# Latent attention: keys of two heads in one product, query weights laid out anew, and the rotary swap in four 32-row corners

## What is computed

```python
MLA_HEADS, MLA_NOPE, MLA_ROPE = 8, 64, 32          # 96 query columns per head
Q_LORA, KV_LORA = 384, 256

def apply_rope(t, cos, sin):
    t1, t2 = jnp.split(t, 2, axis=-1)
    return jnp.concatenate([t1 * cos - t2 * sin, t2 * cos + t1 * sin], axis=-1)

def mla_branch(c_q, c_kv, k_r, cos, sin, q_norm_g, kv_norm_g, w_uq, w_uk, w_uv):
    q = (rmsnorm(c_q, q_norm_g) @ w_uq).reshape(B, S, 8, 96)
    q_nope, q_rope = q[..., :64], apply_rope(q[..., 64:], cos, sin)
    k_rope = apply_rope(k_r, cos, sin)              # one for all heads
    ckv = rmsnorm(c_kv, kv_norm_g)
    k_nope = (ckv @ w_uk).reshape(B, S, 8, 64)
    v = (ckv @ w_uv).reshape(B, S, 8, 64)
    return causal_mla_attention(q_nope, q_rope, k_nope, k_rope, v)
```

## Time and profile before

| | |
|---|---|
| median of 3 runs | 2799.29 us (2795.35 to 2803.37) |
| profiled execution | 2800.07 us, its span 2798.3 us |
| TensorE (PE) | 2739.1 us busy, 21992 matmuls |
| VectorE (DVE) | 1840.9 us busy, 66% |
| ScalarE (ACT) | 1301.3 us busy, 47% |
| GpSimd (POOL) | 70.8 us busy, 3% |
| DMA | 474.50 MB, mean 170 GB/s |

### The profile page before, as it was taken

How to read it: one execution, slowest core, us unless ns; L and a number is a source line. 1 busy time by engine, 2 the same in 40 slices (tenths; PEclk the granted TensorE clock), 3 DMA queues, 4 the chain that set the end, 5 groups by cost and what they waited for, 6 DMA issues and landing times.

```text
span 2798.3 us, 51128 instructions
## 1 busy us (share of the span) xinstructions
PE 2739.1 (98%) x21992; PEld 2601.1 (93%) x21992; DVE 1840.9 (66%) x3008; ACT 1301.3 (47%) x1860; POOL 70.8 (3%) x66
## 2 busy tenths in 40 slices
PE   8999999999999999999999999999999999999998
PEld 8999799999999989999999888899999998878997
DVE  5678676666676666766666557666666654766675
ACT  5445444444444445444544334444464433544443
POOL 0000100000000010000000001100000000110000
PEclk9999999999999999999999999999999999999999
DMA  7554466556546355555565653455555565434553
GB/s 262 189 166 132 128 171 199 183 187 203 195 157 191 97 164 171 177 193 188 193 203 172 191 138 113 99 181 192 189 176 187 181 195 140 135 91 159 193 195 106
DMA packets 481280, 474.50 MB, mean 170 GB/s; under 512 B 47104, under 2 KB 464416, under 8 KB 480928
## 3 DMA queue, kind: packets, MB, share of 16 engines
q1 hardware_dynamic: 477472, 460.75, 52.1%
q0 software_dynamic: 3584, 10.49, 1.4%
HBM read 464.91 MB, written 6.29 MB: 168 GB/s over the span
## 4 chain that ended last, share of the span: by engine, by line
PE 89%; DVE 6%; ACT 3%; DMA 1%; issue 1%; SPq 0%; DVEq 0%; ACTq 0%
PE ps L1059 33%; PE ps L960 32%; PE ps L1080 16%; PE ps L1197 2%; PE ps L1121 2%; DVE WL L1890 2%; PE ps L1166 1%; ACT WH L1511 1%; PE ps L1007 1%; PE ps L1011 1%; PE ps L1003 1%; DMA RAW<-in_w_in 0%; PE ps L991 0%; DMA RAW<-in_w_branch 0%; DVE REGION L2045 0%
## 5 line engine op out<-in xcount | busy, mean ns | idle before, releaser
L1890 DVE TENSOR_TENSOR WL<-RAW,WH 128x2048 fp32r<-128x2048 f32 (+2 forms) x390 | 871.8, 2241 | 459.3 <-ACT WH L1511 457.3
L1511 ACT ACTIVATE WH<-RAW 128x2048 fp32r<-128x2048 f32 (+2 forms) x398 | 737.7, 1867 | 151.7 <-DMA RAW<-in_w_in 83.1
L1080 PE MATMUL ps<-HH,WH 128*128 128x256 f32 x1408 | 388.6, 276 | 0.0
L1080 PE MATMUL ps<-HH,WL 128*128 128x256 f32 x1408 | 388.6, 276 | 0.0
L1080 PE MATMUL ps<-HL,WH 128*128 128x256 f32 x1408 | 388.6, 276 | 0.0
L960 PE MATMUL ps<-UH,WH 128*128 128x256 f32 x1328 | 378.1, 285 | 4.0 <-DVE WL L1890 4.0
L960 PE MATMUL ps<-UH,WL 128*128 128x256 f32 x1328 | 369.7, 278 | 0.0
L960 PE MATMUL ps<-UL,WH 128*128 128x256 f32 x1328 | 369.7, 278 | 0.0
L1059 PE MATMUL ps<-UH,WH 128*128 128x256 f32 x2688 | 363.7, 278 | 0.7 <-DVE WL L1890 0.7
L1059 PE MATMUL ps<-UL,WH 128*128 128x256 f32 x2688 | 361.1, 277 | 0.0
L1059 PE MATMUL ps<-UH,WL 128*128 128x256 f32 x2688 | 360.9, 277 | 0.0
(11 more groups left out here) (326 smaller groups left out, 3696.1 us busy)
## 6 DMA issues: line engine op xcount, KB each, us to landing
RAW<-in_w_ffn_in SPq DMA_DIRECT2D x88, 1024.0 KB, 5.1
RAW<-in_ffn_wi SPq DMA_DIRECT2D x88, 1024.0 KB, 5.1
RAW<-in_w_in SPq DMA_DIRECT2D x86, 1024.0 KB, 5.4
RAW<-in_w_ffn_out SPq DMA_DIRECT2D x32, 1024.0 KB, 4.8
RAW<-in_ffn_wo SPq DMA_DIRECT2D x32, 1024.0 KB, 4.9
RAW<-in_w_out SPq DMA_DIRECT2D x16, 1024.0 KB, 4.9
RAW<-in_w_ffn_out SPq DMA_DIRECT2D x16, 768.0 KB, 4.3
RAW<-in_ffn_wo SPq DMA_DIRECT2D x16, 768.0 KB, 4.2
```

The lines of the kernel that those rows point to most:

```text
L1080: last = nc.tensor.matmul(bank(n + side, 0, T), a[:, k, side * P:(side + 1) * P], b[:, k0 + k, :], start=k0 + k == 0 and a is wh and b is ...
L1511: nc.scalar.activation(split_ap(s, part_high(s)), raw_ap(s), ACT.Copy).then_inc(weights_high, 1)
L1890: v_.tensor_tensor(split_ap(s, part_low(s)), raw_ap(s), split_ap(s, part_high(s)).bitcast(FP), ALU.subtract)\
```

## The change

- The weights `w_uq` are laid out anew ahead of the launch: each half of four heads (384 columns) is now four times 64 position-free columns and then four times 32 rotary ones. So a half is three products of 128 columns: two of two heads' position-free parts, one of four heads' rotary parts.
- `uk` is four products of 128 columns, two heads each. ScalarE evicts such a product in two operations, the upper half moving from partitions 64 to 127 to partitions 0 to 63 (`evict_heads`).
- The rotary parts go to a new tile `QR` of 128 partitions, four heads of 32 rows. The swap is then two products, each of four 32x32 corners with 256 columns in one bank, and the third for the key. The tables stand on all 128 partitions.
- VectorE multiplies with sine and cosine on 128 partitions, and adds into `QH` in four operations, one per head, which read 32 rows from partition 0, 32, 64 or 96 and write to partitions 64 to 95. The squares of `hg.o` come after the first half instead of the second pair.

```diff
@@ constants
     swap = np.zeros((P, ROPE), np.float32)
-    for i in range(ROPE // 2):
-        swap[64 + ROPE // 2 + i, i] = -1.0
-        swap[64 + i, ROPE // 2 + i] = 1.0
+    for r in range(0, P, ROPE):
+        for i in range(ROPE // 2):
+            swap[r + ROPE // 2 + i, i] = -1.0
+            swap[r + i, ROPE // 2 + i] = 1.0
...
-    freq[64:96, 0] = np.concatenate([inv, inv])
+    freq[:, 0] = np.tile(inv, P // len(inv))
@@ make_plan
-        pl.slabs(L + "uq", [4, 4], places=MIX)
+        pl.slabs(L + "uq", [3, 3], places=MIX)
         pl.products(L + f"pairs{LEVELS}", 1)
-        pl.slabs(L + "uk", [8], places=MIX)
+        pl.slabs(L + "uk", [4], places=MIX)
         pl.slabs(L + "uv", [2], places=MIX)
-        pl.products(L + "swap", 5)
+        pl.products(L + "swap", 3)
@@ SP queue
-                sp.dma_start(COS[64:96, :].bitcast(I32), w["pos"]).then_inc(inputs_in, 16)
+                sp.dma_start(COS[:].bitcast(I32), w["pos"]).then_inc(inputs_in, 16)
@@ TensorE
-                    for m in range(4):
-                        n = first[L + "uq"] + 4 * i + m
-                        product(n, [(bank(n)[0:QK, 0:T], [(slot(s, 3, 384)[:, k, m * QK:(m + 1) * QK], CQ[:, k, :]) for k in range(3)])])
+                    for m in range(3):
+                        n = first[L + "uq"] + 3 * i + m
+                        product(n, [(bank(n, 0, T), [(slot(s, 3, 384)[:, k, m * P:(m + 1) * P], CQ[:, k, :]) for k in range(3)])])
...
-                for m in range(MLA_H):
+                for m in range(MLA_H // 2):
                     n = first[L + "uk"] + m
-                    product(n, [(bank(n)[0:NOPE, 0:T], [(slot(s, 2, 512)[:, k, m * NOPE:(m + 1) * NOPE], CKV[:, k, :]) for k in range(2)])])
+                    product(n, [(bank(n, 0, T), [(slot(s, 2, 512)[:, k, m * P:(m + 1) * P], CKV[:, k, :]) for k in range(2)])])
...
-                for m in range(4):
-                    n = first[L + "swap"] + m
-                    product(n, [(bank(n)[64:96, :], [(swap, QH[64:96, 2 * m:2 * m + 2, :])])])
-                n = first[L + "swap"] + 4
-                product(n, [(bank(n)[64:96, 0:T], [(swap, KR[64:96, 0, :])])])
+                for m in range(6):
+                    wait_evicted(pe, first[L + "uq"] + m)
+                for i in range(2):
+                    n = first[L + "swap"] + i
+                    product(n, [(bank(n)[r:r + ROPE, 0:T], [(con("swap", ROPE, slice(r, r + ROPE)), QR[r:r + ROPE, i, :])])
+                                for r in range(0, P, ROPE)])
+                n = first[L + "swap"] + 2
+                product(n, [(bank(n)[64:96, 0:T], [(con("swap", ROPE, slice(64, 96)), KR[64:96, 0, :])])])
@@ ScalarE
+            def evict_heads(n, dst, h):
+
+                wait_product(act, n)
+                nc.scalar.activation(dst[0:NOPE, h, :], bank(n)[0:NOPE, 0:T], ACT.Copy)
+                nc.scalar.activation(dst[0:NOPE, h + 1, :], bank(n)[NOPE:2 * NOPE, 0:T], ACT.Copy).then_inc(evicted[n % BANKS], 1)
...
-                for h in range(MLA_H):
-                    evict(first[L + "uq"] + h, QH[0:QK, h, :], bank(first[L + "uq"] + h)[0:QK, 0:T])
-                for h in range(MLA_H):
-                    evict(first[L + "uk"] + h, KH[0:NOPE, h, :], bank(first[L + "uk"] + h)[0:NOPE, 0:T])
+                for i in range(2):
+                    for m in range(2):
+                        evict_heads(first[L + "uq"] + 3 * i + m, QH, 4 * i + 2 * m)
+                    n = first[L + "uq"] + 3 * i + 2
+                    evict(n, QR[:, i, :], bank(n, 0, T))
+                for m in range(MLA_H // 2):
+                    evict_heads(first[L + "uk"] + m, KH, 2 * m)
@@ VectorE
-                cos2 = COS[64:96, :].unsqueeze(1).broadcast_to([ROPE, 2, T])
-                sin2 = SIN[64:96, :].unsqueeze(1).broadcast_to([ROPE, 2, T])
-                for m in range(4):
-                    if m == 2:
-                        for i in range(2):
-                            wait_evicted(dve, first[L + "hg.o"] + i)
+                for i in range(2):
+                    if i == 1:
+                        for m in range(2):
+                            wait_evicted(dve, first[L + "hg.o"] + m)
                         v_.tensor_tensor(HG_SQ, OT, OT, ALU.mult).then_inc(squares_ready, 1)
                         feed.to(slab_first[L + "hg.gate0"] + 1)
-                    n = first[L + "swap"] + m
-                    q = QH[64:96, 2 * m:2 * m + 2, :]
-                    turned = TMP[64:96, m % 2, :].rearrange("p (g t) -> p g t", g=2)
+                    n = first[L + "swap"] + i
                     wait_product(dve, n)
-                    v_.tensor_tensor(turned, bank(n)[64:96, :].rearrange("p (g t) -> p g t", g=2), sin2, ALU.mult)\
-                      .then_inc(evicted[n % BANKS], 1)
+                    v_.tensor_tensor(TMP[:, i, 0:T], bank(n, 0, T), SIN[:], ALU.mult).then_inc(evicted[n % BANKS], 1)
+                    link(v_.tensor_tensor(QR[:, i, :], QR[:, i, :], COS[:], ALU.mult))
                     wait_evicted(dve, n)
-                    link(v_.tensor_tensor(q, q, cos2, ALU.mult))
-                    link(v_.tensor_tensor(q, q, turned, ALU.add))
-                n = first[L + "swap"] + 4
+                    for j in range(4):
+                        r = slice(j * ROPE, (j + 1) * ROPE)
+                        last = v_.tensor_tensor(QH[64:96, 4 * i + j, :], QR[r, i, :], TMP[r, i, 0:T], ALU.add)
+                    link(last)
+                n = first[L + "swap"] + 2
@@ inputs
+    heads = arrays["w_uq"].reshape(DEPTH, -1, 2, MLA_H // 2, QK)
+    parts = [heads[..., c].reshape(DEPTH, heads.shape[1], 2, -1) for c in (slice(0, NOPE), slice(NOPE, QK))]
+    arrays["w_uq"] = np.ascontiguousarray(np.concatenate(parts, axis=3).reshape(arrays["w_uq"].shape))
```

More of the change, by code:

```diff
@@ L552, in build @@
         MK, MV = region(4, T), region(NT, 512)
-        used[0] = both - 2 * 2 * 2 * 260
+        used[0] = both - 2 * 2 * 2 * 260 - 2 * T
+        QR = region(2, T)
         Z, HK = region(HG_H * T), region(HG_H * T)
@@ L1267, in _ @@
                     tokens(first[L + "uv"] + m, [(bank(first[L + "uv"] + m), lambda k: slot(s, 2, 512)[:, k, :], m)], CKV, 2)
-                swap = con("swap", ROPE, slice(64, 96))
-                for h in range(MLA_H):
-                    wait_evicted(pe, first[L + "uq"] + h)
-                for m in range(4):
-                    n = first[L + "swap"] + m
-                    product(n, [(bank(n)[64:96, :], [(swap, QH[64:96, 2 * m:2 * m + 2, :])])])
-                n = first[L + "swap"] + 4
-                product(n, [(bank(n)[64:96, 0:T], [(swap, KR[64:96, 0, :])])])
+                for m in range(6):
[6 more added lines that the diff above has]
+                product(n, [(bank(n)[64:96, 0:T], [(con("swap", ROPE, slice(64, 96)), KR[64:96, 0, :])])])
                 pe.wait_ge(pairs_summed, l + 1)
@@ L1629, in tables @@
                     act.wait_ge(angle_ready, 1)
-                    nc.scalar.activation(SIN[64:96, :], SIN[64:96, :], ACT.Sin)
-                    nc.scalar.activation(COS[64:96, :], COS[64:96, :], ACT.Sin).then_inc(rope_ready, 1)
+                    nc.scalar.activation(SIN[:], SIN[:], ACT.Sin)
+                    nc.scalar.activation(COS[:], COS[:], ACT.Sin).then_inc(rope_ready, 1)
                 if q == 2:
@@ L2148, in tables @@
                     dve.wait_ge(inputs_in, 32)
-                    link(v_.tensor_copy(V[64:96, :], COS[64:96, :].bitcast(I32)))
-                    link(v_.tensor_scalar(V[64:96, :], V[64:96, :], con("freq", 1, slice(64, 96)), None, ALU.mult))
+                    link(v_.tensor_copy(V[:], COS[:].bitcast(I32)))
+                    link(v_.tensor_scalar(V[:], V[:], con("freq", 1), None, ALU.mult))
                 if q < 2:
                     table, turn = ((SIN, 0.0), (COS, 0.25))[q]
-                    a, n, r = V[64:96, :], TMP[64:96, 0, T:2 * T], table[64:96, :]
+                    a, n, r = V[:], TMP[:, 0, T:2 * T], table[:]
                     link(v_.tensor_scalar(n, a, 1.0 / (2.0 * np.pi), turn, ALU.mult, ALU.add))
@@ L2587 @@
     arrays["pT"] = np.ascontiguousarray(np.asarray(inputs["p_2"])[:, 0].transpose(0, 2, 1))
-    arrays["pos"] = np.ascontiguousarray(np.broadcast_to(np.asarray(inputs["positions"]), (ROPE, T)))
+    arrays["pos"] = np.ascontiguousarray(np.broadcast_to(np.asarray(inputs["positions"]), (P, T)))
     nc = _bacc.Bacc("TRN2", target_bir_lowering=False, num_devices=1)
```

## The result

The changed kernel takes 2780.6 us (median of 4 runs, 2778.05 to 2781.82); the kernel before, run beside it, 2798.6 (2795.35 to 2803.37). The ratio on record is 0.9931, with a 95% interval of 0.9918 to 0.9943 (the two medians alone give 0.9936); so the kernel is faster, clear of noise. The profiled execution took 2780.5 us with a span of 2778.7. Forecast were 2780.0, from 2774 to 2791.

The account below looks back on a forecast made before the run. TensorE, busy 98% of the span, was taken to bound the kernel. Per layer 2.61 + 3.53 + 2.59 + 0.92 = 9.65 us, 19.3 in two layers, so 2799.3 - 19.3 = 2780.0 us, range 2774 to 2791.

Parts of the forecast that it names:

- Query products: TensorE, per layer: 24 query products become 18 at 0.435 us each, 10.44 us to 7.83, -2.61 us.
- Keys: TensorE, per layer: 16 key products become 8 at 0.441 us each, 7.06 us to 3.53, -3.53 us.
- Rotary swap: TensorE, first swap to `hg.o`, per layer: corners overlap fully, 3.97 us to 1.38, -2.59 us.
- Rival 1: TensorE's swap: corners take turns, the stage stays at 3.97 us and the kernel takes 2785.2 us; 22%.
- Evictions on ScalarE: ScalarE, per layer: 16 evictions become 18, partition-moving ones taken at 0.38 us, all hidden behind TensorE's products.
- No wait of weight: ScalarE, first gate slab's high half: its DMA lands near 304.2, the last key eviction ends at about 304.0.
- just fit: ScalarE: SiLU ends 3.2 us after the value products, first `hg.o` eviction ready at 3.0, so the corners' gain just fits.
- Rotation on VectorE: VectorE, per half of the heads: 4.3 us falls to 2.55 with additions at 0.44 us, 1.75 us less on the chain.
- The chain's wait: TensorE's wait for the third gate slab's low half goes in each layer, -0.92 us.
- 0.8 us in hand: VectorE's slack at the third gate slab once TensorE's 0.92 us wait is gone, per layer.
- the forecast's last condition: Forecast is wrong if the stretch shrinks by 9.6 us in each layer but the end does not come 19 us sooner.
- Rivals 2 and 3: 2: a helper holds TensorE later, 2791 us or more, 9%. 3: slow row-changing VectorE additions, 2808 at 2.4 us each, 2%.

Follow-up runs that it names:

- keys alone: Kernel before with only the keys changed (two heads to a product, evicted in two halves): 2794.33 us, ratio 0.9977.
- two more operations ahead of SiLU: Changed kernel with two ScalarE copies of 128x1024, of a tile onto itself, put ahead of SiLU: 2785.15 us, ratio 0.9935.
- low half ahead of the key's copy: Kernel before, with VectorE making the third gate slab's low half before copying the rotated key to all heads: 2797.97 us, ratio 0.9989.
- eight more operations: Changed kernel with eight more linked VectorE multiplications of 32x256 behind the second half's additions: 2788.1 us, ratio 0.9948.
- corners in turns: Changed kernel with the corners within each swap product made to wait for each other by a semaphore: 2788.11 us, ratio 0.9958.

## Why the prediction was right

*Query products.* Right: 18 products at 0.435 us each. 128 columns cost no more than 96, 7.88 / 7.78 us against the 7.83 worked out.

*Keys.* Right in kind, and 0.07 us more than said: 3.45 where I had 3.53. I had taken 0.441 for a product of 64 columns, the stage's length by 16; but inside the stage its records stand 0.216 us apart, as those of 128 columns do, and the rest was at its borders. `pairs8` and `uv` each gave 0.10 us as well, in both layers and in the kernel with the keys alone, and neither in the one that leaves the keys out. They stand on either side of `uk` and are untouched; the gain comes with its 128-column products. The starts of single records show where it is (before, layer 1): the last record of `pairs8` stands 0.205 us ahead of the 64-column keys in place of 0.112, the keys' first and last take 0.267 and 0.309 in place of 0.216, the first of `uv` 0.534 in place of 0.429; after, all four are gone. From the queries' 96 columns to 128 there is no such step. So the cost lies at the change from 128 to 64 columns and back, 0.34 us a layer in all. What TensorE does in that time the traces don't show.

*Rotary swap.* Right: 1.42 us for a forecast of 1.38. The bound of 0.63 us a burst, from the rows of 64, counted entry and drain into every burst, which only the last pays. Rival 1 fell in three ways: four corners start together, corners made to take turns cost 3.4 to 3.6 us more in the stage and 5 to 8 us in the kernel (13.1 us less than before, against 18.0 and 20.7), and one full product costs what four corners do.

The Trainium skill, TensorEngine Tiling (Array Packing), Gotcha 1: PSUM Pressure, says that different row tiles can't use one PSUM bank at the same time. In these runs four row tiles wrote one bank together, each on 32 partitions of its own. As a rule for tiles that don't share partitions it doesn't hold here; tiles that share partitions in one bank were not tried.

*Evictions on ScalarE.* The move from partitions 64 to 127 into 0 to 63 (the first line below) lasts 381 ns against 378 in place, so the forecast's 0.38 was right, and the pair fits behind TensorE.

```profile
L1488 ACT ACTIVATE REGION<-ps 64x256 f32<-64x256 f32 x16 | 6.1, 381 | 0.2
L1487 ACT ACTIVATE REGION<-ps 64x256 f32<-64x256 f32 x16 | 6.0, 378 | 8.4 <-PE ps L962 7.8
```

"No wait of weight" for the first gate slab's DMA was the one sentence that failed in layer 1. I had worked out layer 0 and doubled it, from the median of 5.4 us to landing; there it was 0.35 us late (5.5 from the issue at 302.93 to 308.40), in layer 1 1.64 (6.8 from 966.94 to 973.70). Why it took longer there no run shows. SiLU and the evictions behind it "just fit" in layer 0. In layer 1 the low half of the second gate slab ends at 981.90 + 2.29 = 984.19, and TensorE begins with that slab at 984.42: it fits by some 0.2 us. The end didn't move for it. The two more operations ahead of SiLU show how near that is.

```profile
981.90 2.29 DVE L1901 TENSOR_TENSOR WL<-RAW,WH 128x2048 fp32r<-128x2048 f32 x1 [0.30 <-ACT WH L1519]
...
984.42 0.28 PE L962 MATMUL ps<-UH,WH 128*128 128x256 f32 x1
```

*Rotation on VectorE.* The additions between rows take 0.42 us each, at 0.43 from start to start, where I took 0.44, in the lower part of the range 0.35 to 0.72. They aren't linked, yet they don't stand 0.35 apart as unlinked operations on the same rows do (312.56, 312.89 after); each starts when the one before is through.

The Trainium skill has a rule for that, in VectorE: DVE Perf Modes, Two Vector instructions with no wait between them: an instruction whose input or output starts in another group of 32 partitions than the last one's is held until all earlier ones have finished. The trace agrees: the four additions change the input's group each time and stand 0.43 us apart.

*The chain's wait.* Gone in both layers, and "0.8 us in hand" was measured at 0.4 to 0.8 by operations put in, at the upper end only if idle time is counted. The term was too small: 1.60 / 1.18 us in place of 0.92. The low half ahead of the key's copy gave 1.19 / 1.61 by the same wait alone, so this is not the work of other parts. Of it 1.18 - 0.92 = 0.26 us is what a stop costs beyond the idle time that the row shows. The rows account for it: a record of 0.28 us every 0.118 overlaps its neighbour by 0.16, which the first one behind a stop can't, and the second one then follows after 0.23 (1009.78, 1010.00) in place of 0.118. The other 0.42 comes or stays away with the spacing of the products of the third and fourth gate slabs, 0.113 or 0.118 us from start to start, one of the two through the whole stage but for the piece at the lower clock in the kernel with eight more operations: after has 0.113 in layer 0 and 0.118 in layer 1, the low half ahead of the copy the other way round. The kernel with the keys alone has 0.113 in layer 0 too, with the wait still there. Nothing that I changed picks it; its cause is open.

*The sum.* 9.65 a layer was forecast, 10.52 and 10.13 came, 20.65 us in both, or 20.2 without the 0.42 that came by the spacing. What is beyond 19.3 is the borders (0.27 a layer: 0.10, 0.10 and 0.07) and the stops (0.26 a layer), less 0.15 in the queries and the swap of both layers. The medians differ by 18.0 in the first batch of runs that has both kernels, and by 20.7 in the other. The spans of the two profiled executions differ by 19.6; the stretch began 4.1 us later in the one after. In the ten profiles with the larger tables it begins at 291.84 to 294.86, in the three with the tables as before at 290.77, 291.39 and 293.90. So the larger set-up of the tables, for which I took nothing and at most 0.5 us, can't be told from what executions differ in anyway. So 2780.6 for 2780.0 is nearer than the forecast had a right to: the terms were 0.9 us short, and medians of the kernel before differ by 2.7 us and more between the first batch and the others. By the letter of the forecast's last condition, an end that does not come 19 us sooner, the first batch's 18.0 would speak against it and the other's 20.7 for it; runs that lie 4 to 8 us apart can't decide a microsecond.

*Rivals 2 and 3.* Nothing of the saving was waited for later: no wait of TensorE in the stretch, and `hg.out` as long as before. Additions between rows cost 0.42 us, far from the 1.9 from which the third would decide.

## What to carry to other kernels

Four small products in different row groups and column groups of TensorE cost together what one costs, even into one PSUM bank, when each has 32 partitions of its own (eight corners 0.90 us); a padded block-diagonal matrix does the same with one instruction, so choose by what is simpler. A float32 product costs by its moving columns (0.432 us for 256), with weights 32, 64, 96 or 128 columns wide, so fill the width first, and pay for it with evictions that change partitions, which on ScalarE cost what those in place do (381 ns and 378). When an engine is sped up, look in each layer by itself at which DMA comes next: a load that was 0.35 us late in one layer was 1.6 us late in the other, and there used up nearly all slack behind it.

## What the runs showed of the hardware that I had not expected

Behind a long stage of 32x32 products, one at a time, the granted clock fell to the lower of its two levels in 4 of 8 places (both layers of four kernels: the kernel before in neither, keys alone in layer 0, corners in turns in both, low half ahead of the copy in layer 0). Each cost 1.4 to 1.7 us, most of it in `hg.o`. In 18 places where the stage is 1.0 to 1.5 us long (nine profiles of seven kernels) it did not fall. TensorE counts as busy all through the long stage and is granted 1.00 in it until its last records. Whether the shape of the products there or the length of the stage is the reason was not tested. Pieces at the lower level stand elsewhere in the program too, near 200 us in three of the thirteen profiles and not in the others, so executions differ by them. In some executions this would be one more gain of the change; the kernel before has it in neither layer of its profile, so it is no part of the 20.65 us, and how often it comes in runs without a profile is not known.

A fifth 32x32 tile that shares its rows of the array with one corner and its columns with another started 0.05 us behind the four and overlapped them: 1.00 us for nine products of 256 columns, where one alone in turn takes 0.52. It started ahead of four products that stand before it in the program and whose tiles were taken. So products to different tiles can start in another order than the program's. By the trace, where ends of products are modelled, the key's records ended at 308.26 too, and the corners' at 308.66.
